# A three-part model on one core: the compressed attention layers rebuilt (order of the weight chunks, values as the stationary side, probabilities normalised one step ahead, norms from token sums)

## Chip, cores, metric

One core of one Trainium2 chip. The metric is the device time of one execution in microseconds; 3497.52 us is the median of three executions of the kernel before (3493.31 to 3498.54).

## What is computed

x has 512 tokens of 1024 features. Two layers of a first block (a gated mixer with attention, a linear attention layer, each with a feed-forward part) are followed by two layers of a second block. Only the middle part of a second-block layer matters here:

```python
x = x + 0.5 * rms(swiglu(rms(x), ...))                  # feed-forward 1
h = hybrid_mixer(rms(x))
x = x + rms(h)
x = x + 0.5 * rms(swiglu(rms(x), ...))                  # feed-forward 2

def hybrid_mixer(h):
    q, kc, vc, ks, vs, kw, vw, gates, bg, cg, xc = split(h @ w_in)
    # q: 8 heads x 64, in 2 groups of 4; each k, v: 2 groups x 64; bg, cg, xc: 512
    kc, vc = compress(kc), compress(vc)   # 31 blocks of 32 tokens: gelu(block @ w1) @ w2
    o_cmp = softmax(q . kc, blocks that ended) @ vc
    o_slc = softmax(rope(q) . rope(ks), causal) @ vs     # all 8 blocks are selected at 512 tokens
    o_win = softmax(rope(q) . rope(kw), causal) @ vw     # window of 512 tokens
    attn = g0 * o_cmp + g1 * o_slc + g2 * o_win          # g = sigmoid(gates)
    conv = bg * conv3(cg * xc)
    return concat(rms(attn), rms(conv)) @ w_out
```

## The kernel before

Everything is kept transposed: features on the 128 partitions, 512 tokens along them. A weight matrix is cut into chunks of 1024 x 256. SyncE loads chunks into a ring of four (line 2277); ACT rounds each into a high part (`split_next`, line 631), GpSimd subtracts for the low part (`low_part`, line 2297) and TensorE makes three products for each of 8 row tiles and 2 column tiles, 48 in all (`chunk_products`, line 451). h is split into high and low in the same way. ACT asks for its splits in an order that is written out by hand, two chunks ahead of TensorE, so a wait ahead of a split in ACT's queue holds the ring. A result sits in one of two two-bank PSUM buffers (`ps`) until DVE has taken it (`take`, line 1999); two more double banks (`mp`, single banks `m[0]` to `m[3]`) are for the rest.

The norm of x is not applied to h: its reciprocal root multiplies the results. Token sums of the squares (line 484) give a column, ACT takes the root, DVE the reciprocal and four diagonal tiles (line 748), and products with ones spread it over the partitions (line 500). `first_chunk` (lines 540 to 544) multiplies one chunk while the tiles of h arrive; the feed-forward layers use `first_pair` (lines 520 to 525), two chunks at once, the second into `mp[1]`.

`nsa_tensor`, `nsa_scalar` and `nsa_vector` are the compressed attention layer on TensorE, ACT and DVE. ACT first issues seven DMAs (lines 1860 to 1866), for which it waits until x is complete. The chunks then come in this order: kc/vc, ks/vs, cg/xc twice (columns 0 to 255, then 256 to 511), q first half, compression of k (two chunks, line 1621), kw/vw, q second half, bg twice, compression of v, gates (one column tile, 24 products), w_out. Between them stand the rotations (`turn_k`, `turn_q`, line 1660), transposes of v (`turn_v`, line 1653), the conv in DVE's `conv`, and the conv half's norm, made with wide products against ones (line 1852).

The attention itself runs in 24 steps over (query tile i, head pair m, branches): tiles 3 and 2 take one branch a step with 128(i+1) keys for each of two heads, tiles 1 and 0 both branches. In a step TensorE makes scores (line 1676) and adds the mask (line 1680), DVE finds the row maximum (line 2177), ACT the exponential (line 1962), TensorE transposes the probabilities (line 1692), ACT copies the first head's from PSUM (line 1971) and DVE the second's (line 2199), and TensorE multiplies with the values (line 1710):

```python
last = pe.matmul(out[:, u * (HD + 1):(u + 1) * (HD + 1)],
                 c.b_pT[:, s % 2, hh, t * P:(t + 1) * P], c.b_va[:, br, j, hh, :], ...)
```

The transposed probabilities are the stationary side; the values carry a column of ones, so that column 65 is the denominator. DVE's `combine` divides, gates and adds into token-major `b_o`. Turns lag scores by one step, values by two. At the end ACT squares each tile of `b_o` with an accumulated sum (lines 1981, 1984), and diagonal tiles turn, scale and transpose it back by products (line 1833) for the output projection (line 1820).

The first block's attention (line 956) has the values as stationary side already: for each tile j, head 0 into output partitions 0 to 63, then head 1 into 64 to 127. Its exponentials write a sum with `accum_out` (line 980). Lines 1098 and following have the same shape, one head after the other.

## Time and profile before

| what | value |
|---|---|
| median of three executions | 3497.52 us |
| the profiled execution | 3496.36 us |
| its span, first to last instruction | 3494.6 us |
| mean granted TensorE clock | 0.969 |
| TensorE, GpSimd, DVE, ACT busy | 3322.8, 1449.9, 1220.3, 1145.4 us |
| first compressed attention layer, h arriving to last step | 1702.0 to 1984.5 us |
| the second one's steps | 2961.7 to 3060.1 us (98.4, the first one's 97.7) |

Times inside are microseconds from the start of the span. A matmul with float32 operands is recorded as two matmuls; a record lasts longer than the distance to the next, because matmuls overlap, so distances between starts are what counts. The granted clock is 1.00 at 2.4 GHz and 0.50 at 1.2 GHz.

### The profile page before, as it was taken

To read this page: it belongs to the slowest core of one execution; us is meant where nothing else is said; L and a number is where in the kernel's file an instruction comes from. 1 tells how busy PE (TensorE), PEld (TensorE's weight loads), DVE (VectorE), ACT (ScalarE), POOL (GpSimd) and SP (SyncE) were. 2 spreads that over 40 slices of the span, in tenths; PEclk is the share of its full clock that TensorE was granted. 3 is DMA by queue.
4 is the path that set the end of the run, shared out by engine and by line. 5 is a ranking of instruction groups with operands and counts; after the bars stand their busy time and mean duration, and the time that the engine had idled before them with its cause. 6 is when DMAs were issued, how large, how long until landed. Compare 5 with 4: busy or idle time off the path is not lost.

```text
span 3494.6 us, 38964 instructions
## 1 busy us (share of the span) xinstructions
PE 3322.8 (95%) x15612; PEld 2716.9 (78%) x15612; DVE 1220.3 (35%) x1681; ACT 1145.4 (33%) x1203; POOL 1449.9 (41%) x1112
## 2 busy tenths in 40 slices
PE   8869999988799999999889999999999989999998
PEld 7638888866588888888777888888888767888887
DVE  6243432132643311220544652214221363752212
ACT  4244432241243323322323443223332223433321
POOL 4204554522155445445353054444544355035443
PEclk9959999988899999999999999999999999999999
DMA  4102222311022232222222022232222223012222
GB/s 147 63 0 85 96 96 107 104 71 60 24 97 96 96 109 97 96 96 103 100 97 73 9 89 96 96 109 86 97 97 105 85 94 121 1 73 96 96 97 96
DMA packets 46224, 302.04 MB, mean 86 GB/s; under 512 B 5392, under 2 KB 7696, under 8 KB 10784
## 3 DMA queue, kind: packets, MB, share of 16 engines
q1 hardware_dynamic: 41040, 292.79, 23.4%
q10 hardware_dynamic: 5072, 7.57, 0.7%
q8 instruction: 93, 1.52, 0.2%
q14 instruction: 19, 0.16, 0.0%
HBM read 296.15 MB, written 2.10 MB: 85 GB/s over the span
## 4 chain that ended last, share of the span: by engine, by line
PE 90%; DVE 5%; issue 3%; ACT 2%; ACTq 0%; DMA 0%; DVEq 0%; SPq 0%
PE main L451 73%; PE misc L1710 2%; PE main L561 2%; PE main L1820 1%; PE main L1676 1%; PE misc L1692 1%; PE main L1621 1%; PE main L520 1%; DVE diag L748 1%; PE main L521 1%; PE main L525 1%; PE misc L520 1%; PE misc L521 1%; PE misc L525 1%; PE main L1680 1%
## 5 line engine op out<-in xcount | busy, mean ns | idle before, releaser
L2297 POOL TENSOR_TENSOR w_lo<-stage,w_hi 128x512 fp32r<-128x512 f32 x1104 | 1444.6, 1341 | 2008.7 <-ACT w_hi L631 2008.5
L451 PE MATMUL main<-h_hi,w_lo 128*128 128x512 f32 x2616 | 1032.4, 395 | 18.9 <-DVE b_u L1999 18.9
L451 PE MATMUL main<-h_lo,w_hi 128*128 128x512 f32 x2616 | 1024.0, 391 | 0.0
L451 PE MATMUL main<-h_hi,w_hi 128*128 128x512 f32 x2616 | 1023.8, 391 | 0.0
L631 ACT ACTIVATE w_hi<-stage 128x2048 fp32r<-128x2048 f32 x276 | 525.2, 1910 | 462.3 <-DMA stage<-in_w 447.6
L451 PEld LDWEIGHTS main<-h_hi,w_lo 128*128 128x128 f32 x2616 | 495.6, 189 | 128.8 <-DVE b_u L1999 19.4
L451 PEld LDWEIGHTS main<-h_lo,w_hi 128*128 128x128 f32 x2616 | 495.7, 189 | 104.8 <-issue 2.4
L451 PEld LDWEIGHTS main<-h_hi,w_hi 128*128 128x128 f32 x2616 | 494.8, 189 | 104.2
L451 PE MATMUL main<-hid_hi,w_lo 128*128 128x512 f32 x1168 | 455.6, 390 | 0.2 <-DVE hid_lo L1537 0.2
L451 PE MATMUL main<-hid_lo,w_hi 128*128 128x512 f32 x1168 | 454.6, 389 | 0.0
L451 PE MATMUL main<-hid_hi,w_hi 128*128 128x512 f32 x1168 | 454.5, 389 | 0.0
L451 PEld LDWEIGHTS main<-hid_hi,w_lo 128*128 128x128 f32 x1168 | 219.5, 188 | 46.8 <-issue 0.7
L451 PEld LDWEIGHTS main<-hid_lo,w_hi 128*128 128x128 f32 x1168 | 219.4, 188 | 46.2 <-issue 0.5
L451 PEld LDWEIGHTS main<-hid_hi,w_hi 128*128 128x128 f32 x1168 | 219.4, 188 | 45.3
L820 DVE TENSOR_TENSOR val<-main,rstd 128x1024 f32<-128x1024 f32 x60 | 73.4, 1224 | 460.8 <-PE main L451 460.8
L800 DVE TENSOR_TENSOR gate<-main,rstd 128x1024 f32<-128x1024 f32 x66 | 80.8, 1224 | 318.0 <-PE main L451 301.2
L684 ACT ACTIVATE hid_hi<-val 128x1024 f32 (+1 forms) x66 | 69.9, 1059 | 370.6 <-DVE val L826 370.6
L853 DVE TENSOR_SCALAR y<-main,par 128x512 f32<-128x512 f32 x48 | 36.0, 750 | 389.8 <-PE main L451 330.7
L830 DVE TENSOR_TENSOR hid_lo<-val,hid_hi 128x1024 f32 (+1 forms) x66 | 89.5, 1356 | 91.1 <-ACT hid_hi L684 91.1
L679 ACT ACTIVATE sq<-gate 128x1024 f32<-128x1024 f32 x44 | 46.7, 1061 | 186.7 <-DVE gate L818 186.2
L845 DVE TENSOR_TENSOR x<-main,x 128x1024 f32<-128x1024 f32 x16 | 19.6, 1224 | 240.6 <-PE main L451 240.6
L1962 ACT ACTIVATE b_p<-main,b_nmax 128x512 f32<-128x512 f32 (+3 forms) x128 | 58.7, 525 | 92.2 <-DVE b_nmax L2177 92.2
(364 smaller groups left out, 3012.9 us busy)
## 6 DMA issues: line engine op xcount, KB each, us to landing
stage<-in_w SPq DMA_DIRECT2D x276, 1024.0 KB, 4.8
x<-in_xT SPq DMA_DIRECT2D x4, 512.0 KB, 8.3
out_x<-x ACTq DMA_DIRECT2D x4, 512.0 KB, 2.7
stage<-in_w SPq DMA_DIRECT2D x4, 256.0 KB, 8.4
b_r<-sq ACTq DMA_DIRECT2D x4, 256.0 KB, 3.5
b_r<-sq ACTq DMA_DIRECT2D x4, 255.5 KB, 4.5
ev_ws<-in_ev_ws ACTq DMA_DIRECT2D x1, 512.0 KB, 3.6
b_pos<-in_pos ACTq DMA_DIRECT2D x2, 256.0 KB, 4.7
```

The costliest lines, as they stand in the source:

```text
L451: last = pe.matmul(acc[:, m, :], w[a], r[b], start=start and k == 0 and j == 0, stop=stop and k == nk - 1 and j == 2)
L520: pe.matmul(accs[j][:, m, :], w[1], c.h_hi[:, k, :], start=k == 0, stop=False)
L521: pe.matmul(accs[j][:, m, :], w[0], c.h_hi[:, k, :], start=False, stop=False)
L525: last = pe.matmul(accs[j][:, m, :], c.w_hi[:, slots[j], k, m * P:(m + 1) * P], c.h_lo[:, k, :], start=False, stop=k == KT - 1)
L561: last = pe.matmul(acc[:, m, :], w[a], r[b], start=start and k == 0 and j == 0, stop=k == nk - 1 and j == 2)
L631: act.activation(c.w_hi[:, s, :, :].rearrange("p k n -> p (k n)"), c.stage[:, s, :], ACT.Copy)\
L684: e.activation(two(c.hid_hi, i), c.val[:, :, :], ACT.Copy).then_inc(c.hid_hi_done, 1)
L800: e.tensor_tensor(c.gate[:, :, 2:], c.ps[n.slot()][:, :, :], rstd, ALU.mult)\
L820: e.tensor_tensor(c.val[:, :, :], (c.mp[1] if extra else c.ps[n.slot()])[:, :, :], rstd, ALU.mult)\
L830: e.tensor_tensor(two(c.hid_lo, i), c.val[:, :, :], two(c.hid_hi, i).bitcast(F32), ALU.subtract).then_inc(c.hid_lo_done, 1)
L1710: last = pe.matmul(out[:, u * (HD + 1):(u + 1) * (HD + 1)], c.b_pT[:, s % 2, hh, t * P:(t + 1) * P], c.b_va[:, br, j, hh, :], start=brs[0] ...
L2297: last = e.tensor_tensor(c.w_lo[:, s, k:k + 2, :].rearrange("p k n -> p (k n)"), c.stage[:, s, k * CW:(k + 2) * CW], c.w_hi[:, s, k:k + 2, ...
```

## The change

- Chunks: kc/vc, cg first half, ks/vs, xc first half, compression of k, q first half, compression of v, kw/vw, gates, q second half, cg and xc second halves, bg twice, w_out with its first 512 rows reordered. The first two go through `first_pair`. ACT's splits and the steps of DVE and TensorE are reordered to match. `b_h` and `b_u` get two buffers.
- Values: `b_va` (64 columns, no ones) is the stationary side, the transposed probabilities stream, two heads go to the two halves of the output partitions, and all steps of a query tile and its compressed part add up in one PSUM bank.
- Probabilities: the exponential writes the denominators (`accum_out`), DVE's `shares` scales the probabilities by gate / denominator before their transposes. Turns lag scores by two steps, values by three. Both heads' copies are ACT's. A group of steps ends with one copy and two squares on ACT.
- Norms of both halves: token sums, root, diagonal tiles and a spread, the conv half's inside the steps.

```diff
-        self.b_p, _ = at("b_p", [2, 2, T], M2)
+        self.b_p, _ = at("b_p", [3, 2, T], M2)
-        self.b_va, _ = at("b_va", [2, TT, 2, HD + 1], MH)
+        self.b_va, _ = at("b_va", [2, TT, 2, HD], MH)
...
     def values(s):
...
+        pe.wait_ge(c.a_copied, 50 * l + 2 * s + 4)
+        for r, br in enumerate(brs):
+            for j in range(i + 1):
+                t = r * (i + 1) + j
+                for hh in range(2):
+                    last = pe.matmul(c.m[2 + i % 2][HD * hh:HD * hh + HD, m * P:(m + 1) * P],
+                                     c.b_va[:, br, j, hh, :], c.b_pT[:, s % 2, hh, t * P:(t + 1) * P],
...
+    def compressed_values(i):
...
+        for m in range(4):
+            for hh in range(2):
+                pe.matmul(c.m[2 + i % 2][HD * hh:HD * hh + HD, m * P:(m + 1) * P], c.b_vbd[:, hh, m, :],
+                          c.b_pcT[:, hh, i * P:(i + 1) * P], start=m == 0, stop=False)
+    def half_sums():
+        pe.wait_ge(c.half_sq, n(c.half_sq, 2))
+        for k in range(4):
+            last = token_sums(pe, c.m[2], c.ones, (c.sq, c.val)[k // 2][:, k % 2, :], k == 0, k == 3)
...
+    first_pair(pe, n, c, [group_slot(pe, n, c), extra_slot(n, c)])
+    chunk_products(pe, n, c, slot_after_extra(pe, n, c), c.h_hi, c.h_lo, KT, at={1: lambda: spread(pe, n, c)})
+    chunk_products(pe, n, c, slot_after_extra(pe, n, c), c.h_hi, c.h_lo, KT)
     pe.wait_ge(c.turn_loaded, 16 * (l + 1))
     turn_k()
     turn_v()
+    compressed(0)
+    z()
+    pe.wait_ge(c.tok_copied, n(c.tok_copied))
+    compressed_turn(0)
+    compressed(1)
+    rope_was_read()
+    turn_q(0)
+    compressed_out(0)
+    z()
...
+    z()
+    pe.wait_ge(c.a_gate_exp, l + 1)
+    turn_q(1)
+    rope_was_read()
+    pe.wait_ge(c.tok_copied, n(c.tok_copied))
+    compressed_scores()
+    z()
+    compressed_prob_turn()
     z()
     z()
...
+    for s in range(N_STEPS + 3):
         if s < N_STEPS:
             scores(s)
+        if s == 3:
+            half_sums()
+        if s == 6:
+            half_spread()
+        if 2 <= s < N_STEPS + 2:
+            turn(s - 2)
+        if s >= 3:
+            if group_starts(s - 3):
+                compressed_values(STEPS[s - 3][0])
+            values(s - 3)
...
+    half(accs[0], slots[0], 4, True, False, at={6: o_sums})
     pe.wait_ge(c.w_lo_done, n(c.w_lo_done))
+    half(accs[1], slots[1], 4, True, False, at={5: o_spread})
...
     split_next(act, n, c)
+    split_next(act, n, c)
     norm_copy(act, n, c)
-    split_next(act, n, c)
...
+    split_next(act, n, c)
+    split_next(act, n, c)
+    trig(c.b_cos)
     rounded(0)
     split_next(act, n, c)
     rounded(1)
+    token_values(0)
+    split_next(act, n, c)
+    gelu(0)
+    split_next(act, n, c)
+    trig(c.b_sin)
...
+    for s in range(N_STEPS + 4):
+        if s >= 4 and group_ends(s - 4):
...
+            act.activation(c.b_oT[:, :, i * P:(i + 1) * P], bank, ACT.Copy)
+            for j in range(2):
+                last = act.activation((c.sq, c.val)[j][:, :, i * P:(i + 1) * P], bank[:, 2 * j:2 * j + 2, :],
+                                      ACT.Square)
...
+        if 2 <= s < N_STEPS + 2:
...
+            for hh in range(2):
+                act.wait_ge(c.a_probT, 50 * l + 2 * s - 2 + hh + 1)
+                act.activation(c.b_pT[:, (s - 2) % 2, hh, 0:w], c.m[hh][:, 0:w], ACT.Copy).then_inc(c.a_copied, 1)
...
+                                   ACT.Exp, bias=c.b_nmax[:, s % 4, u:u + 1],
+                                   accum_out=c.b_den[:, s % 4, 2 * hh + br:2 * hh + br + 1]).then_inc(c.a_prob, 1)
+        if s == 2:
+            act.wait_ge(c.conv_done, n(c.conv_done))
+            for j in range(2):
+                act.activation((c.sq, c.val)[j][:, :, :], c.b_y[:, 2 * j:2 * j + 2, :], ACT.Square)\
+                    .then_inc(c.half_sq, 1)
+        if s == 4:
+            act.wait_ge(c.half_ssq, n(c.half_ssq))
+            act.activation(c.col[:, 0:4], c.m[2][:, 0:4], ACT.Sqrt, bias=c.eps, scale=1.0 / 512)\
+                .then_inc(c.half_std, 1)
...
     norm_recip(dve, n, c)
     take(c.sq[:, :, :])
     signal(c.kc_taken)
+    take(c.b_u[0][:, :, :], extra=True)
...
     dve.wait_ge(c.pairs_loaded, n(c.pairs_loaded, 64))
     flat(0)
+    flat(1)
+    take(c.val[:, :, :])
+    conv(0)
+    hidden(0)
+    angle(c.b_sin, 0.0)
...
+    take(c.b_u[1][:, :, :])
+    rope_q(1)
...
+    def shares(s):
...
+        dve.wait_ge(c.a_prob, 64 * l + exps_until(s + 1))
...
+        step(dve.reciprocal(den, den))
+        step(dve.tensor_tensor(den, den, gate, ALU.mult))
+        for hh in range(2):
+            for r, br in enumerate(brs):
+                p = c.b_p[:, s % 3, hh, r * w:(r + 1) * w]
+                u = 2 * hh + br
+                last = dve.tensor_scalar(p, p, c.b_den[:, s % 4, u:u + 1], None, ALU.mult)
+            last.then_inc(c.a_norm, 1)
```

## Rows read from the trace of the kernel before

**Rows 1.** The page, busy time, share of the span and instructions of each engine.
```profile
PE 3322.8 (95%) x15612; PEld 2716.9 (78%) x15612; DVE 1220.3 (35%) x1681; ACT 1145.4 (33%) x1203; POOL 1449.9 (41%) x1112
```

**Rows 2.** Stretches: start, end, length, busy time by engine, granted clock, DMA share, GB/s.
```profile
1731.98:1886.80 154.82, 142.69 (x698) 115.85 (x696) 72.86 (x87) 44.23 (x42) 80.73 (x57) 0.95 0.30 103
1886.80:1984.53 97.73, 92.44 (x699) 76.74 (x698) 71.05 (x144) 47.46 (x105) 4.01 (x4) 0.98 0.03 11
1984.53:2011.38 26.85, 26.85 (x129) 22.67 (x130) 9.01 (x21) 9.64 (x12) 7.16 (x6) 0.95 0.11 40
```

**Rows 3.** The chain of waits, in order of time: start, length, what.
```profile
1807.09 5.62 PE main L1621 x48
...
1814.43 10.90 PE main L451 x48
...
1872.00 3.45 PE misc L1852 x8
```

**Rows 4.** Timeline, front of the first layer: start, length, instructions, idle before and releaser.
```profile
1701.99 0.47 PE L540 MATMUL main<-h_hi,w_lo 128*128 128x512 f32 x1 [0.34 <-ACT h_hi L730]
...
1720.09 0.95 PE L484 MATMUL misc<-ones,acc 128*128 128x1 f32 x8
...
1724.14 1.91 ACT L631 ACTIVATE w_hi<-stage 128x2048 fp32r<-128x2048 f32 x1 [6.96 <-issue]
...
1726.13 4.92 POOL L2297 TENSOR_TENSOR w_lo<-stage,w_hi 128x512 fp32r<-128x512 f32 x4 [38.40 <-ACT w_hi L631]
...
1726.45 4.68 DVE L748 TENSOR_SCALAR diag<-ident,col 128x128 f32<-128x128 f32 x4
```

**Rows 5.** Timeline, front of the feed-forward layer behind it, TensorE.
```profile
2040.29 0.47 PE L520 MATMUL main<-h_hi,w_lo 128*128 128x512 f32 x1 [0.34 <-ACT h_hi L730]
...
2063.07 0.40 PE L451 MATMUL main<-h_hi,w_lo 128*128 128x512 f32 x1
```

**Rows 6.** Timeline, the long wait of the projections on three engines.
```profile
1763.28 0.60 ACT L1885 ACTIVATE b_va<-misc 128x512 f32<-128x512 f32 x1 [9.81 <-PE misc L1653]
...
1766.70 1.37 DVE L2057 TENSOR_TENSOR b_a_lo<-b_flat,b_a_hi 128x992 fp32r<-128x992 f32 x1 [11.91 <-ACT b_a_hi L1890]
...
1772.72 0.79 PE L451 MATMUL main<-h_hi,w_lo 128*128 128x512 f32 x1 [9.48 <-DVE b_u L1999]
```

**Rows 7.** Timeline, a step of query tile 3, and one of tile 1 on ACT.
```profile
1911.79 1.26 ACT L1962 ACTIVATE b_p<-main,b_nmax 128x512 f32<-128x512 f32 x2 [2.31 <-DVE b_nmax L2177]
...
1912.94 0.60 ACT L1971 ACTIVATE b_pT<-misc 128x512 f32<-128x512 f32 x1
...
1913.06 1.13 PE L1676 MATMUL main<-b_k,b_qr 64*128 64x512 f32 x4
...
1914.39 1.06 PE L1692 MATMUL misc<-ident,b_p 128*128 128x128 f32 x8
...
1915.29 1.90 PE L1710 MATMUL misc<-b_va,b_pT 128*128 128x65 f32 x16
...
1917.12 1.13 PE L1676 MATMUL main<-b_k,b_qr 64*128 64x512 f32 x4
...
1962.28 1.57 ACT L1962 ACTIVATE b_p<-main,b_nmax 128x256 f32<-128x256 f32 x4 [1.79 <-DVE b_nmax L2177]
```

**Rows 8.** Groups by line and shape over 1720 to 2023: count, busy us, mean ns, idle before.
```profile
L1710 PE MATMUL misc<-b_va,b_pT 128*128 128x65 f32 x320 | 38.6, 272 | 0.4 <-issue 0.4
```

**Rows 9.** Timeline and a stretch (last row), the first block's attention and mixing.
```profile
168.68 1.34 PEld L1098 LDWEIGHTS misc<-ev_ws,ev_vntok 128*64 128x64 f32 x16 [0.18 <-DVE val L1238]
...
256.73 0.18 ACT L980 ACTIVATION_READ_ACCUMULATOR score<-score,stat 128x1 f32 x1
...
261.56 1.09 PE L956 MATMUL misc<-probT,vs 128*64 128x128 f32 x16 [0.74 <-ACT probT L987]
262.59 0.50 PE L451 MATMUL main<-hid_hi,w_lo 128*128 128x512 f32 x1
...
183.00:262.00 79.00, 56.58 (x288) 31.95 (x290) 32.83 (x162) 35.40 (x93) 0.00 (x0) 0.58 0.00 0
```

More of the change, by code:

```diff
@@ L1661, in turn_q, with rope_was_read, gates_turn @@
         last.then_inc(c.rope_ps, 1)
+    def rope_was_read():
+        pe.wait_ge(c.rope_read, n(c.rope_read))
+    def gates_turn():
+        pe.wait_ge(c.gates_taken, n(c.gates_taken))
+        for t in range(TT):
+            last = pe.transpose(c.m[1][:, t * 24:(t + 1) * 24], c.acc[0:24, 0, t * P:(t + 1) * P],
+                                c.ident[0:24, 0:24])
+        last.then_inc(c.gates_turned, 1)
     def scores(s):
@@ new lines, in half_sums, with half_spread @@
+    def half_sums():
+        pe.wait_ge(c.half_sq, n(c.half_sq, 2))
+        for k in range(4):
+            last = token_sums(pe, c.m[2], c.ones, (c.sq, c.val)[k // 2][:, k % 2, :], k == 0, k == 3)
+        last.then_inc(c.half_ssq, 1)
+    def half_spread():
+        pe.wait_ge(c.half_diag, n(c.half_diag))
+        for i in range(TT):
+            last = pe.matmul(c.m[2][:, i * P:(i + 1) * P], c.ones[:, :], c.diag[:, i, :], start=True, stop=True)
+        last.then_inc(c.half_spread, 1)
+    first_pair(pe, n, c, [group_slot(pe, n, c), extra_slot(n, c)])
@@ L1815, in half @@
+        if 2 <= s < N_STEPS + 2:
[4 more added lines that the diff above has]
+            values(s - 3)
+    def half(acc, s, k0, start, stop, at={}):
         for k in range(k0, k0 + 4):
+            if k in at:
+                at[k]()
             for m in range(2):
@@ L1822, in half, with o_sums, o_spread @@
         return last
+    def o_sums():
+        pe.wait_ge(c.a_oT, 4 * l + 4)
+        for k in range(4):
+            last = token_sums(pe, c.m[0], c.ones, (c.sq, c.val)[k // 2][:, k % 2, :], k == 0, k == 3)
+        last.then_inc(c.half_ssq, 1)
+    def o_spread():
+        pe.wait_ge(c.half_diag, n(c.half_diag))
+        for i in range(TT):
+            last = pe.matmul(c.m[1][:, i * P:(i + 1) * P], c.ones[:, :], c.diag[:, i, :], start=True, stop=True)
+        last.then_inc(c.half_spread, 1)
     c.result_slot[post] = n.slot()
@@ L1845, in nsa_tensor @@
     last_sums(pe, n, c)
-def half_norm_tensor(pe, n, c):
-    for j in range(2):
-        pe.wait_ge(c.half_sq, n(c.half_sq))
-        for k in range(2):
-            last = pe.matmul(c.m[0][:, :], c.ones[:, :], (c.sq, c.val)[j][:, k, :],
-                             start=j == 0 and k == 0, stop=j == 1 and k == 1)
-    last.then_inc(c.half_ssq, 1)
 def nsa_scalar(act, n, c, l, norm, post, a, out):
@@ L2081, in hidden, with gated @@
         signal(c.cmp_taken)
-    def conv_gate(j):
-        take(c.val[:, :, :])
+    def gated(j):
         y = c.b_y[:, 2 * j:2 * j + 2, :]
@@ L2173, in nsa_vector @@
+    for s in range(N_STEPS + 1):
         if s < N_STEPS:
@@ new lines, in nsa_vector @@
+            signal(c.conv_done)
+        if s >= 1:
+            shares(s - 1)
+        if s == 5:
+            dve.wait_ge(c.half_std, n(c.half_std))
+            step(dve.reciprocal(c.col[:, 0:4], c.col[:, 0:4]))
+            for i in range(TT):
+                last = dve.tensor_scalar(c.diag[:, i, :], c.ident[:, :], c.col[:, i:i + 1], None, ALU.mult)
+            last.then_inc(c.half_diag, 1)
+        if 7 <= s < 9:
+            if s == 7:
+                dve.wait_ge(c.half_spread, n(c.half_spread))
+            x = c.b_y[:, 2 * s - 14:2 * s - 12, :]
+            dve.tensor_tensor(x, x, over_tiles(c.m[2][:, :]), ALU.mult).then_inc(c.half_done, 1)
```

450 lines of the change are left out of this document (153 added, 297 removed).

## The prediction

> **What bounds the kernel now.** I began with the page: TensorE is busy for 95% of the span and every other engine for 41% or less [rows 1]. So time comes back only where TensorE does less, works at the lower clock level or stands still. The change touches the two compressed attention layers alone, so next I cut the first of them into stretches: the projections before the attention steps, the 24 steps, and the first part of the output projection [rows 2]. The projections last 154.8 us with TensorE busy for 142.7 (12.1 us of standing still) at a mean granted clock of 0.95. The steps last 97.7 us with 92.4 busy at 0.98. The tail has no standing still. The second layer runs the same code with the same shapes. One execution of a layer is therefore 280 us of TensorE's queue, and twice anything found there is the answer.
>
> The chain of waits gives prices: 48 products of a weight chunk take 10.90 us (0.227 us each), the two compression chunks together 5.62, the conv half's norm through four wide ones-products 3.45 [rows 3].
>
> **Front of the layer.** Today one chunk is multiplied while h arrives. TensorE starts it at 1702.0; ACT issues seven DMAs after x is complete and splits the next chunk only at 1724.1; GpSimd makes its low part from 1726.1 in 4.92 us; DVE's four diagonal tiles take 4.68 us, ending at 1731.1, and the norm is spread by 1732.0 [rows 4]. Until then TensorE has done 66 products (48, and 18 of the second chunk). The change takes two chunks at once, as the feed-forward layers do: there the pair runs from 2040.3 to 2063.1, 22.8 us, with the sums inside [rows 5]. So here TensorE is through at 1702.0 + 22.8 = 1724.8, with 96 products done. But the third chunk is the one that ACT splits at 1724.1 behind its DMAs, and its low part is ready at 1726.1 + 4.9 = 1731.0: 6.2 us of standing still. Then 6 products (2.6 us, since it restarts at the lower level) and the spread (about 1.4): 1735.0. ACT now splits two chunks ahead of the square root, which moves the diagonals 1.9 us later, to 1733.0, still ahead of the spread. Net: the mark is 3.0 us later, with 102 products behind it and not 66; the 36 extra are 8.2 us. Gain 5.2 us. What the feed-forward layer has and this one doesn't is the ready third chunk; I do not give it that.
>
> **From the norm to the first step.** The 154.8 us hold one long wait, 9.48 us before the products of line 451, released by DVE's b_u. Behind it is a circle: DVE had waited 11.91 us for ACT's rounding of the compression blocks, and ACT was held 9.81 us in its order at the transposed values of TensorE's line 1653 [rows 6]. The change breaks this: both roundings stand ahead of the transposed values in ACT's queue and both compressions' inputs ahead of the sine angles in DVE's. So the 9.5 us go, and with them about 1.5 us of lower clock behind the pause. Work: 154.8 less 12.1 of standing still less about 4.7 lost at the lower level (0.95 over the stretch) is 138.0. From this go the 36 products that are now ahead of the mark (8.2) and the wide norm products (3.45); the turn of the compressed probabilities comes in (0.9). That is 127.2. What is late next? Walking the queues with the rows' durations I find: the second compression chunk of v or the key products near 1780, where GpSimd has 5.3 us a chunk and TensorE eats two in 5.62 (0 to 2 us); the values' transposes behind ACT's four copies (0.6); and the compressed scores, which wait for DVE's last rotation, itself behind the conv input that is now taken just before (2.0 to 2.6). With some lower clock I put 5 us: 132.2, ending 132.2 + 3.0 = 135.2 after today's mark. Against 154.8 the gain is 19.6 us, the front's 5.2 included.
>
> The cover for the compression is the weight ring. Splits are now asked for in pairs on ACT, and two compressions stand with only one 48-product chunk between them. Five chunks cost GpSimd 5 x 5.3 = 26.5 us while TensorE works about 2.8 x 4 + 11 x 2 = 33: it holds, with some 1 us of margin at the tightest.
>
> **The 24 steps.** A step of the last query tile runs 1913.06 to 1917.12, 4.06 us, TensorE never standing: scores and mask 1.33, transposes 0.90, values 1.83 [rows 7]. Values change form: now 128 columns of probabilities are loaded and 65 columns streamed; then 64 columns of values are loaded and 128 streamed, two heads into the two halves of the output partitions. The first attention layer already does this: 16 records from 261.56 to the next product at 262.59, 1.03 us. The same 64-column load without the alternation took 1.34 us of loads for 16 records. These are the two ends; I take the first, the same form in the same order [rows 9]. Saved: (1.83 - 1.03) / 16 x 320 records = 16.0 us a layer [rows 8]. The Trainium skill (TensorEngine Tiling (Array Packing), Key Properties) says that a change of tiling mode drains TensorE, which speaks against the change, since the values become a third form in each step. The row of 1.03 us already holds one such change at its end, so the trace bears the rule out only as something below 0.2 us a step.
>
> Other work of TensorE there: compressed values become 32 small products, 4 x 1.03 = 4.1 for 3.4 today; the conv norm now stands inside as 16 token sums, four of which take about 0.8 us [rows 4], so 3.3, and a spread of 0.9; the turn leaves (0.9). Busy today 92.4, less 2.0 for the lower level, is 90.5; so 90.5 - 16.0 + 0.7 + 4.2 - 0.9 = 78.5.
>
> That would be 19 us of gain, and I don't expect most of it. ACT gets DVE's half of the copies (about 12.7 us), 64 accumulator reads at 0.19 [rows 9] (12.2), the squares of the conv half (2.1), copies and squares of four groups (7), and two function table loads in step 4 (2.6). A step of tile 3 costs ACT two exponentials (1.26, 0.38 for reads) and two copies (0.55 apiece, a little under the row's 0.60, since they overlap), 2.7 in all, against TensorE's 3.26: covered. Tile 1: four exponentials took 1.57 [rows 7]; 2.4 with reads, and copies 1.1: 3.5 against 3.5. Tile 0: 2.7 against 2.2: ACT is the bound. DVE has 2.6 at most. TensorE's pauses in the walk: 2.0 at the third scores, 3.5 at the token sums (they wait for ACT's squares, which wait for DVE's gating), 0.7 at the spread, 3.3 spread over the ACT-bound steps, 5.0 in the longer drain (values now three steps behind scores). Together 14.5; with 1 us of clock the steps last 94.0 against 97.7. Gain 3.7 us.
>
> **Tail.** 16 wide products become 16 sums and a spread (3.3 + 0.9 for 3.6). DVE and ACT then make four tiles of hid in turn, each 1.4 us, as fast as TensorE takes them. Loss 0.5 us.
>
> **Sum.** 19.6 + 3.7 - 0.5 = 22.8 a layer, 45.6 for two. The profiled execution took 3496.4 us (span 3494.6), 1.2 below the median of three, 3497.5; so about 3451 for that, the forecast of the likeliest case.
>
> **Rivals.** (a) *The steps stay at ACT's or the column form's pace.* At 1.34 us for the values form, the walk gives 3 us more a layer; if an accumulator read costs 0.3 and not the 0.23 of the walk, 3.3 more. One or both: 3451 + 6 to 13, about 3462, and the steps give nothing. For: ACT is level with TensorE in eight steps. Against: row of 1.03. (b) *The ring starves.* DVE and GpSimd hold each other up more; my walk lengthens each DVE operation on SBUF beside GpSimd by 1.0 us (a diagonal tile beside it takes 4.68 / 4 = 1.17 us [rows 4]); with 1.4 it gives 6.7 us more a layer: 3464. (c) *The queues fit better.* No pause at the sums, reads hidden: the steps take 86, the projections 130: 10 us less a layer, 3431. (d) *The clock falls in the steps: slower.* The first attention layer, with the same pattern of short pauses, ran its 79 us at 0.58 [rows 9], most of it at 1.2 GHz, against 2.4 GHz in today's steps. If the new pauses (15% of the stretch, where today's are 5%) do this, the 78.5 us of work double. The point from which it decides is 22.8 / 78.5 = 29% of the work at the lower level, which eats the gain; all of it, with the 14.5 us of pauses swallowed by the longer work, makes 2 x (78.5 - 14.5 - 22.8) = 82 more than today, 3579. For: that row. Against: today's last steps pause too and stay near full clock. (e) *The order gives nothing*, because a new wait of 13 us takes the place of the b_u wait and the steps gain nothing: 2 x (19.6 - 13) = 13, 3484.
>
> **How the numbers follow.** Forecast 60%, (a) 12%, (b) 8%, (c) 9%, (d) 5%, (e) 6%. A measurement of this kernel can tell about 0.2%, 7 us, from no change. Faster holds all but (d) and part of (e): 0.91; same 0.04, slower 0.05. The range takes in (a), (b) and most of (c), and the bounds of the values form: 3430 to 3474.
>
> **What would show it.** Right: no wait above 3 us for b_u or val before line 451; about 6 us of standing still ahead of the third chunk; first step's scores 17 to 22 us earlier relative to the layer's start; value records 0.06 us apart; steps of tile 3 at 3.3 us, of tile 0 released by ACT; clock 0.95 or more. Wrong: TensorE released by GpSimd's low parts in the middle; a granted clock near 0.5 in the steps; steps of tile 3 released by ACT.

## The result, and the profile after

The changed kernel takes 3465.4 us, median of four runs (3463.1 to 3465.9), against 3498.0 for the kernel before: a ratio of 0.9909, 95% interval 0.9895 to 0.9922, a gain of 32.6 us. The forecast was 3451, the range 3430 to 3474. The direction is right and the range holds it; 14 us of the forecast gain are missing. The number by itself doesn't choose between the forecast and its rivals: it lies nearer to (a), about 3462, and (b), 3464, than to 3451. What chooses is the profile, and the runs further down.

The page of the changed kernel, to be read against [rows 1]:

```profile
span 3463.6 us, 39458 instructions
...
PE 3308.1 (96%) x15788; PEld 2697.2 (78%) x15788; DVE 1205.3 (35%) x1689; ACT 1185.4 (34%) x1395; POOL 1447.2 (42%) x1112
```

TensorE's busy time fell by 14.7 us and its standing still from 171.8 to 155.5, by 16.3. The stretches of the first compressed layer, cut at the same events as [rows 2] with the front ahead of them (start, end, length, busy time of PE, PEld, DVE, ACT and POOL, granted clock, DMA share, GB/s):

```profile
1701.24:1734.46 33.22, 26.88 (x118) 22.13 (x119) 21.95 (x31) 12.73 (x14) 8.95 (x8) 0.90 0.26 90
1734.46:1874.96 140.50, 133.62 (x663) 108.87 (x661) 77.92 (x90) 43.93 (x45) 79.07 (x57) 0.96 0.30 105
1874.96:1966.81 91.85, 87.50 (x777) 65.21 (x777) 60.02 (x150) 67.00 (x196) 0.00 (x0) 0.93 0.04 13
1966.81:1994.83 28.02, 28.02 (x138) 23.80 (x137) 7.86 (x15) 8.75 (x12) 7.03 (x6) 0.94 0.10 38
```

| us, first layer | before | forecast | after |
|---|---|---|---|
| first h product to the spread norm | 30.0 | 33.0 | 33.2 |
| from there to the first scores | 154.8 | 132.2 | 140.5 |
| the 24 steps | 97.7 | 94.0 | 91.9 |
| tail | 26.9 | 27.4 | 28.0 |

From one layer's first h product to the next's it is 322.65 and 323.25 us in the two layers, 15.65 and 14.60 less than before; forecast was 22.8. The projections are short by 8.3, the tail by 0.6, and the steps give 2.1 more.

TensorE's waits of the first layer, timeline of the changed kernel (start, length, group, idle time ahead of it and its releaser):

```profile
1730.58 0.76 PE L444 MATMUL main<-h_hi,w_lo 128*128 128x512 f32 x1 [6.34 <-POOL w_lo L2276]
...
1764.10 0.50 PE L444 MATMUL main<-h_hi,w_lo 128*128 128x512 f32 x1 [2.02 <-DVE val L2004]
...
1781.77 0.33 PE L1612 MATMUL main<-w_hi,b_a_lo 128*62 128x256 f32 x1 [1.68 <-POOL w_lo L2276]
...
1788.58 0.47 PE L444 MATMUL main<-h_hi,w_lo 128*128 128x512 f32 x1 [1.10 <-POOL w_lo L2276]
...
1833.88 4.72 PE L1715 MATMUL misc<-b_kc,b_q 64*128 64x32 f32 x64 [1.45 <-DVE b_qr L2040]
...
1879.33 1.13 PE L1676 MATMUL main<-b_k,b_qr 64*128 64x512 f32 x4 [1.41 <-ACT b_p L1971]
...
1886.92 2.28 PE L477 MATMUL misc<-ones,sq 128*128 128x1 f32 x13 [1.85 <-ACT val L1978]
```

The 9.48 us for b_u [rows 6] are gone; instead of it four short waits stand in the projections, 6.25 us, and 0.6 in two smaller ones. Behind the wait for val, behind the one for b_qr and in the first steps the granted clock is lower for a while. Behind the two waits for GpSimd's low parts it is not: it stays at 1.00 from 1776 to 1836, and in the second layer, where the first of them is 2.74 us long, from 2837 to 2852 too. The same kernel in finer stretches:

```profile
1764.00:1768.00 4.00, 3.90 (x11) 3.03 (x12) 3.89 (x4) 0.72 (x1) 4.00 (x3) 0.60 0.58 236
1776.00:1836.00 60.00, 55.15 (x292) 43.65 (x292) 24.97 (x32) 20.73 (x24) 43.01 (x32) 1.00 0.35 123
1836.00:1842.00 6.00, 6.00 (x38) 5.26 (x37) 2.40 (x3) 0.00 (x0) 0.00 (x0) 0.54 0.00 0
1842.00:1850.00 8.00, 8.00 (x34) 6.51 (x34) 4.45 (x5) 2.86 (x2) 4.69 (x3) 0.92 0.00 0
1887.00:1892.00 5.00, 5.00 (x27) 5.00 (x28) 0.51 (x2) 0.00 (x0) 0.00 (x0) 0.57 0.01 3
1892.00:1897.00 5.00, 5.00 (x34) 4.67 (x36) 0.00 (x0) 2.50 (x6) 0.00 (x0) 0.50 0.00 0
1897.00:1966.00 69.00, 68.34 (x680) 50.87 (x676) 49.51 (x131) 57.01 (x175) 0.00 (x0) 0.99 0.01 2
```

A step of query tile 3, as in [rows 7]:

```profile
1901.64 1.13 PE L1676 MATMUL main<-b_k,b_qr 64*128 64x512 f32 x4
1902.70 0.44 PE L1680 MATMUL main<-b_mask,b_identr 128*128 128x128 f32 x2
1902.97 1.06 PE L1691 MATMUL misc<-ident,b_p 128*128 128x128 f32 x8
1903.96 1.09 PE L1702 MATMUL misc<-b_pT,b_va 128*64 128x128 f32 x16
1904.99 1.13 PE L1676 MATMUL main<-b_k,b_qr 64*128 64x512 f32 x4
```

3.35 us instead of 4.06: values 1.03 instead of 1.83, transposes 0.99 instead of 0.90.

### The profile page after: what moved, and what is told of

Same layout as the page of the kernel before. It is cut to its first block, busy times and chain, and to the rows that moved or that the text cites. A ratio compares the mean times of both kernels' runs of the same rounds, so it can differ in the third digit from the quotient of the medians.

```text
span 3463.6 us, 39458 instructions
## 1 busy us (share of the span) xinstructions
PE 3308.1 (96%) x15788; PEld 2697.2 (78%) x15788; DVE 1205.3 (35%) x1689; ACT 1185.4 (34%) x1395; POOL 1447.2 (42%) x1112
## 4 chain that ended last, share of the span: by engine, by line
issue 49%; POOL 32%; PE 17%; DVE 1%; ACT 1%; POOLq 0%; DMA 0%; ACTq 0%; DVEq 0%; SPq 0%
POOL w_lo L2276 32%; PE main L444 12%; PE main L1815 1%; PE main L554 1%; PE main L1676 1%; PE misc L1702 1%; PE misc L1691 0%; PE misc L477 0%; DVE h_lo L2337 0%; PE main L1680 0%; DMA stage<-in_w 0%; PE misc L1715 0%; ACT b_p L1971 0%; DVE y L879 0%; POOLq L2274 0%
## 5 line engine op out<-in xcount | busy, mean ns | idle before, releaser
L444 PE MATMUL main<-h_hi,w_lo 128*128 128x512 f32 x2584 | 1017.9, 394 | 17.3 <-POOL w_lo L2276 13.9
L444 PE MATMUL main<-h_lo,w_hi 128*128 128x512 f32 x2584 | 1012.0, 392 | 0.0
L444 PE MATMUL main<-h_hi,w_hi 128*128 128x512 f32 x2584 | 1011.7, 392 | 0.0
L819 DVE TENSOR_TENSOR val<-val,sq 128x1024 f32<-128x1024 f32 x66 | 86.4, 1309 | 7.8
```

The lines of the kernel that those rows point to most:

```text
L444: last = pe.matmul(acc[:, m, :], w[a], r[b], start=start and k == 0 and j == 0, stop=stop and k == nk - 1 and j == 2)
L819: e.tensor_tensor(c.val[:, :, :], c.val[:, :, :], c.sq[:, :, :], ALU.mult)\
```

## The experiments

Each run changes the kernel after the change in one place, conv_late in two (it holds take_early's early value chunk) and best_four in four. Medians are compared with its 3465.4 us; the layer columns are the distance of first h products in the profiled run.

| run | median, us | ratio to before (95%) | layer 1 | layer 2 |
|---|---|---|---|---|
| the change | 3465.4 | 0.9909 (0.9895 to 0.9922) | 322.65 | 323.25 |
| splits_first | 3447.8 | 0.9863 (0.9848 to 0.9878) | 315.76 | 313.79 |
| take_early | 3467.4 | 0.9917 (0.9903 to 0.9932) | 322.77 | 323.42 |
| conv_late | 3454.6 | 0.9878 (0.9862 to 0.9893) | 315.73 | 317.36 |
| scores_late | 3457.5 | 0.9895 (0.9880 to 0.9910) | 319.29 | 316.97 |
| sums_late | 3459.9 | 0.9895 (0.9880 to 0.9910) | 318.84 | 317.37 |
| best_four | 3425.2 | 0.9796 (0.9782 to 0.9811) | 304.63 | 303.41 |
| undo_pair | 3474.1 | 0.9934 (0.9920 to 0.9947) | 326.06 | 326.56 |
| token_form | 3501.1 | 1.0014 (1.0003 to 1.0026) | 341.42 | 346.09 |
| heads_outer | 3480.3 | 0.9954 (0.9942 to 0.9967) | 331.50 | 328.82 |
| copy_in_four | 3463.5 | 0.9916 (0.9900 to 0.9931) | 326.13 | 320.66 |
| fill_pause | 3462.2 | 0.9896 (0.9880 to 0.9911) | 321.94 | 317.95 |
| fill_whole | 3467.5 | 0.9910 (0.9894 to 0.9927) | 322.56 | 324.13 |

A single layer of a single profile scatters with the clock: in copy_in_four the part ahead of the steps, where nothing differs, took 177.3 us against 173.7, at 0.92 against 0.95. So the medians judge and the profiles say where. The executions of one kernel lie 3 to 16 us apart, and an interval reaches some 5 us either way, so a difference of 2 or 3 us between medians says nothing.

**splits_first: ScalarE's splits ahead of its DMA issues.**

```diff
+    split_next(act, n, c)
+    split_next(act, n, c)
+    n.skip(c.acc_ready, 2)
+    norm_std(act, n, c)
     act.wait_ge(c.nsa_free, n(c.nsa_free))
     act.dma_start(c.b_pos[:, :], a["pos"]).then_inc(c.pos_loaded, 16)
...
-    split_next(act, n, c)
-    split_next(act, n, c)
-    norm_copy(act, n, c)
+    act.wait_ge(c.spread_ready, n(c.spread_ready))
+    act.activation(c.rstd[:, :], c.m[1][:, :], ACT.Copy).then_inc(c.rstd_copied, 1)
```

> The changed kernel with ScalarE's two weight splits (and the square root) put ahead of its wait for the layer's memory and its seven DMA issues. Theory (the front's pause is ScalarE's order, nothing else): ScalarE stood 7.09 us ahead of the split at 1723.52, so the splits come some 7 us earlier, GpSimd's low part of the third chunk too, and TensorE's wait for it (6.34 us in layer 1, 5.38 in layer 2) is gone but for up to 0.5 us in front of the spread: 11 us less, 3454 against 3465. Rival (GpSimd and the ring of weight buffers set the pace, so that time won in one place is lost in the next wait for a low part): the pause at the third chunk shrinks and the waits for w_lo near 1781 and 1788 grow by as much; 3463 to 3466. Rival 2 (TensorE's granted clock gives back what the pause cost, the chip allowing only so much work): the pause goes and the share of the higher clock in the layer falls; less than half of the 11 us.

17.6 us less, more than the 11 expected. The pause is gone and with it the low clock of the front, which the 11 had left out: the norm is spread 25.4 us after the first h product, in both layers, and not 33.2 and 32.6. In the run:

```profile
1724.00:1728.00 4.00, 4.00 (x19) 3.33 (x20) 2.77 (x4) 0.60 (x1) 2.22 (x2) 1.00 0.90 329
1728.00:1730.60 2.60, 2.60 (x14) 2.13 (x13) 2.43 (x9) 0.31 (x2) 0.00 (x0) 1.00 1.03 340
1730.60:1733.00 2.40, 2.40 (x12) 2.01 (x11) 2.30 (x4) 2.40 (x3) 0.00 (x0) 1.00 1.03 220
```

The changed kernel has 0.24 us of TensorE in the first of these stretches, 0.02 in the second, and in the third a clock of 0.50. Both rivals fall: the waits for w_lo further on grew by only 0.5 us (2.17 and 1.11 in layer 1), and the wait for val from 2.02 to 3.22, which is far less than the 7.8 us won in front of them; and the clock of the steps didn't fall, it rose (0.94 for 0.93).

**take_early and conv_late: VectorE's order.** The diff is that of take_early; in conv_late `conv(0)` stands further down, between `hidden(1)` and `rope_q(0)`.

```diff
     flat(0)
+    take(c.val[:, :, :])
     flat(1)
-    take(c.val[:, :, :])
-    conv(0)
     hidden(0)
+    conv(0)
     angle(c.b_sin, 0.0)
```

> The changed kernel with VectorE's order in the projections altered: the gate's value chunk is scaled out of PSUM after the first of the two flattening groups instead of after both, and the first compressed hidden group is taken before the convolution instead of after it. Theory (the 8.3 us by which the projections missed the forecast are short waits on in-order neighbours, and a lower clock behind each): the wait for val at 1764.10 (2.02 us; 1.38 in layer 2) goes, with it the low clock behind it (that chunk took 12.71 us against 10.93, 1.8 us); the GELU is no longer 8.64 us late, so the split behind it is 5 us or more earlier and TensorE's waits for GpSimd's w_lo near 1781 and 1788 (1.68 and 1.10 us; 2.74 and 1.10 in layer 2) go too: 5 to 7 us a layer, 3452 to 3456. Rival (GpSimd's pace): the w_lo waits stay, only the first wait and its clock go: 3 us a layer, 3459. Rival 2 (the clock's loss is not tied to these waits): val's wait goes but the low stretch turns up elsewhere: 1.5 to 4 us in all.

> Like the run with the value chunk taken early, where the wait of 2.02 us for val went and one of 3.47 us for the scaled queries came in its place, but with the convolution's first half (some 9 us of VectorE) put behind the scaling of the queries and the second hidden group. Theory (between 1745 and 1787 VectorE's own chain is the bound, and what is moved inside it only moves the wait): with 9 us taken out of the chain both waits go, and the low clock behind the first (1.8 us): 3.5 to 4.5 us a layer, 3456 to 3458; GpSimd's two waits (2.0 and 1.1 us) stay. Rival (the convolution is then late for the rotation of the queries and the second turning of the keys, near 1805): a new wait of 2 to 4 us there, 3462 to 3466.

take_early gave nothing, which neither theory nor rivals had. The wait for val and its low clock went, but in its place:

```profile
1787.55 3.75 PE L1650 MATMUL misc<-b_q,b_turn 128*128 128x512 f32 x4 [3.47 <-DVE stat L2011]
```

With the convolution taken out of the chain (conv_late) this wait is gone too, the one for val doesn't return, and 10.8 us are won, more than the 8 expected. So VectorE's chain from the flattening to the scaled queries was the bound there, and shuffling inside it only moved the wait. Of the 10.8 us, 5.0 are waits (the projections' are 2.0 and 3.0 us shorter in the two layers). Most of the rest is clock, and not all of that can be laid to the edit: behind the wait for b_qr, 1.45 us as before, the low stretch of its first layer is half as long. GpSimd's two waits stayed (1.77 and 1.34). No new wait stands near 1805.

**scores_late: compressed scores one chunk later.** ScalarE's third split goes ahead of its exponential of them.

```diff
     turn_q(1)
+    z()
     rope_was_read()
     pe.wait_ge(c.tok_copied, n(c.tok_copied))
     compressed_scores()
     z()
     compressed_prob_turn()
     z()
-    z()
```

> The changed kernel with the compressed scores and the transposes of their probabilities one chunk later on TensorE, so that VectorE's rotation of the second half of the queries is over before the scores want the bank. Theory: the wait of 1.45 us for b_qr (both layers) goes and the clock no longer falls behind it (scores 4.65 against 3.70 before the change, masks 1.02 against 0.57, the chunk 12.66 against 10.93: 3.1 us); if all of that is tied to the wait, 4.5 us a layer, 3456. Rival (the scores themselves, narrow products of 32 columns, lower the clock behind them, not the wait): 1.5 us a layer, 3462. Rival 2 (the later end of VectorE's work on the compressed probabilities delays the convolution and the last two scalings out of PSUM): a new wait in front of the first scores or of the last chunk, 3465 or more.

7.9 us less, between the two prices. The wait is gone, the scores take 3.69 us instead of 4.65. In the first layer the clock still falls behind them, for a shorter time:

```profile
1842.00:1848.00 6.00, 6.00 (x72) 5.33 (x71) 0.00 (x0) 0.00 (x0) 0.56 (x1) 0.89 0.49 175
1848.00:1856.00 8.00, 8.00 (x32) 6.51 (x32) 6.67 (x8) 1.06 (x1) 0.00 (x0) 0.87 0.01 2
```

Counting 1 minus the granted clock times the length, that is 1.7 us lost against 3.4 in the two stretches from 1836 to 1850 of the changed kernel. In the second layer it doesn't fall at all (1.00 from 2899 to 2913). So the low stretch doesn't need the wait, since it can come without it, here and in both layers of best_four; what share the narrow products have in it isn't settled.

**sums_late: the convolution half's norm two steps later.**

```diff
-        if s == 3:
+        if s == 5:
             half_sums()
-        if s == 6:
+        if s == 8:
             half_spread()
```

ScalarE's and VectorE's parts of it move by two steps as well.

> The changed kernel with the convolution half's token sums, spread, scaling and low parts two steps later in the attention loop. Theory (the one long pause in the steps, 1.85 us for val in front of the sums, 2.49 in layer 2, is the squares not being ready at the fourth step): the pause is gone or under 0.3 us and the low clock of 1887 to 1897 with it: 2 us and some 2 of clock a layer, 3457. Rival (the low clock is brought on by the first steps themselves, which follow the chunks, with small products): only the pause goes, 3461. Rival 2 (ScalarE is the bound of the first steps): the pause moves to the next step's exponentials, 3465.

5.5 us by the medians, between the prices of theory and rival. The wait for val is gone; the steps last 88.44 and 88.42 us in the two layers, for 91.85 and 93.46. A low stretch at the first steps remains (0.72 from 1886 to 1892), shorter than before, but a second one stands around the sums' new place:

```profile
1898.00:1908.00 10.00, 10.00 (x63) 8.45 (x63) 2.23 (x6) 2.53 (x6) 0.00 (x0) 0.66 0.00 0
```

So of the low clock the larger part moved along with the sums, and what went is mainly the wait.

**best_four: the four edits together** (splits_first, conv_late, scores_late, sums_late).

> The changed kernel with the four edits together: splits first, convolution late (with the early value chunk), scores late, sums late. Alone they gave, against the changed kernel's 3465.4: 17.6, 10.8, 7.9 and 5.5 us by the medians, 41.8 together. Theory (each removes a wait of its own and the lower clock behind it, in different places of the layer): they add up but for the clock of the first steps, which three of them counted as theirs (2.4 us in layer 2): 3424 to 3430. Rival (GpSimd's pace: with the layer's front 6 us earlier and the projections' waits gone, the low parts of the compressed and query chunks come late): two or more of the gains go into waits for w_lo, 3435 to 3445.

3425.2 us, as the theory had it: 40.2 less than the change, where the four alone sum to 41.8. What is left of waits for other engines in its first layer, up to the steps (timeline; beside them 1.02 us at 1747.28 that the profile puts down to no engine, and 0.28 for b_vbd):

```profile
1753.63 0.47 PE L444 MATMUL main<-h_hi,w_lo 128*128 128x512 f32 x1 [0.55 <-POOL w_lo L2279]
...
1769.74 0.33 PE L1612 MATMUL main<-w_hi,b_a_lo 128*62 128x256 f32 x1 [1.73 <-POOL w_lo L2279]
...
1776.24 0.47 PE L444 MATMUL main<-h_hi,w_lo 128*128 128x512 f32 x1 [1.35 <-POOL w_lo L2279]
...
1865.51 1.13 PE L1676 MATMUL main<-b_k,b_qr 64*128 64x512 f32 x4 [1.40 <-ACT b_p L1974]
```

This version beats both kernels, the one before by 2.0% (1.9 to 2.2). That the four nearly add up says that they stand in different places; it doesn't show each one's mechanism.

**undo_pair: the front as before.**

```diff
-    first_pair(pe, n, c, [group_slot(pe, n, c), extra_slot(n, c)])
-    chunk_products(pe, n, c, slot_after_extra(pe, n, c), c.h_hi, c.h_lo, KT, at={1: lambda: spread(pe, n, c)})
-    chunk_products(pe, n, c, slot_after_extra(pe, n, c), c.h_hi, c.h_lo, KT)
+    first_chunk(pe, n, c, group_slot(pe, n, c))
+    chunk_products(pe, n, c, group_slot(pe, n, c), c.h_hi, c.h_lo, KT, at=norm_hooks(pe, n, c))
+    z()
+    z()
...
```

ScalarE's copy of the spread and VectorE's second scaling move with it.

> The changed kernel with the front undone: one chunk alone under the activations, token sums and spread inside the second, VectorE's second scaling out of an ordinary bank, ScalarE's copy of the spread between its two splits. Theory: 36 of the 102 products that now lie ahead of the spread move behind it (8.2 us at 0.227 us each) and the pause ahead of the third chunk, with the low clock behind it, goes (the mark at 30.0 instead of 33.2 us after the first product): 5 us a layer more, 3475 against 3465. Rival (the pair is worth nothing, because GpSimd's low parts, which start as late either way, hand the gain back further on): within 2 us of 3465. Rival 2 (the front's pause is what the pair costs, and the undone form is the better one by it): 3455 to 3460.

8.6 us more, where 10 were expected: that bears out the front's term of 5.2 us a layer, as near as runs that scatter by 7 us can. In the profile the first scores come 3.4 and 5.3 us later after the first h product, and some of that is clock.

**token_form and heads_outer: the value products.** First token_form's edit, then the order of the loops in heads_outer.

```diff
-                    last = pe.matmul(c.m[2 + i % 2][HD * hh:HD * hh + HD, m * P:(m + 1) * P],
-                                     c.b_va[:, br, j, hh, :], c.b_pT[:, s % 2, hh, t * P:(t + 1) * P],
+                    last = pe.matmul(c.m[2 + i % 2][:, m * P + HD * hh:m * P + HD * hh + HD],
+                                     c.b_pT[:, s % 2, hh, t * P:(t + 1) * P], c.b_va[:, br, j, hh, :],
...
```

```diff
-        for r, br in enumerate(brs):
-            for j in range(i + 1):
-                t = r * (i + 1) + j
-                for hh in range(2):
+        for hh in range(2):
+            for r, br in enumerate(brs):
+                for j in range(i + 1):
+                    t = r * (i + 1) + j
```

> The changed kernel with the products of probabilities and values, and the compressed ones, in the form of the kernel before (probabilities stationary, 64 columns of values moving, tokens on the partitions of the output); copies and squares read the bank as they did, so what comes out is in another arrangement and only the time is of use. Theory (the steps are bound by TensorE, and the value form is worth 0.8 us for each 16 products, 1.83 against 1.03): 20 times 0.8 us, 16 us a layer more, less 0.1 us a step for the change of form that falls away: 13 to 16 us a layer, 3491 to 3498, the whole gain of the change again. Rival (ScalarE's copies and exponentials set the pace of the steps): the products grow but run in what were waits; 3 to 8 us a layer, 3471 to 3481.

> The changed kernel with the value products of a step in another order: all of the first head, then all of the second, instead of one head and the other in turn (the two write different halves of the output's partitions). Theory (the alternation is what gives 1.03 us for 16 records; without it the nearest row of the kernel before had 1.34 us of loads for 16): 0.3 us for each 16 records, 6 us a layer, 3477 to 3479 against 3465. Rival (the pace is that of one product, 128 columns streamed, whatever its place): no change, 3464 to 3467. Rival 2 (nothing at all overlaps without the alternation, and a product takes twice as long): 20 us a layer, 3505.

token_form costs 35.6 us, the whole gain and more; the rival (ScalarE sets the pace) falls. The profiled execution took 3508.9 us. The step's values take 1.82 us again, from 1906.84 to 1908.66. Part of the excess over 32 is clock. Stretches of its second layer's steps:

```profile
2963.00:2973.00 10.00, 8.98 (x46) 8.99 (x46) 0.90 (x3) 2.28 (x5) 0.00 (x0) 0.58 0.00 0
2973.00:2983.00 10.00, 10.00 (x42) 8.38 (x43) 1.34 (x3) 1.71 (x5) 0.00 (x0) 0.50 0.01 2
2983.00:2993.00 10.00, 10.00 (x43) 8.38 (x42) 4.30 (x13) 6.13 (x12) 0.00 (x0) 0.50 0.01 2
2993.00:3003.00 10.00, 10.00 (x54) 7.55 (x54) 2.44 (x6) 3.79 (x10) 0.00 (x0) 0.71 0.00 0
3003.00:3013.00 10.00, 10.00 (x83) 8.78 (x81) 8.50 (x17) 6.58 (x17) 0.00 (x0) 1.00 0.01 2
```

heads_outer costs 14.9 us, near the theory's 12 to 14. Its step:

```profile
1901.06 1.06 PE L1691 MATMUL misc<-ident,b_p 128*128 128x128 f32 x8
1902.05 1.58 PE L1702 MATMUL misc<-b_pT,b_va 128*64 128x128 f32 x16
1903.56 1.13 PE L1676 MATMUL main<-b_k,b_qr 64*128 64x512 f32 x4
```

1.51 us for the 16 records in place of 1.03: in a step of tile 3 the alternation of the two heads is worth 0.48 us of the form's 0.80. In a step of tile 2, with 12 records, it is 1.07 for 0.81, so the steps are 7.5 us longer in each layer and not 20 times 0.48.

**copy_in_four: does ScalarE bind the last steps?**

```diff
-    act.activation(c.b_pT[:, (s - 2) % 2, hh, 0:w], c.m[hh][:, 0:w], ACT.Copy).then_inc(c.a_copied, 1)
+    parts = 4 if s - 2 >= 16 else 1
+    for q in range(parts):
+        x = slice(q * w // parts, (q + 1) * w // parts)
+        last = act.activation(c.b_pT[:, (s - 2) % 2, hh, x], c.m[hh][:, x], ACT.Copy)
+    last.then_inc(c.a_copied, 1)
```

> The changed kernel with ScalarE's copies of the transposed probabilities cut into four instructions each in the last eight steps of a layer (what is copied is the same); by the distance of ScalarE's short instructions, some 0.2 us from one to the next, it adds about 0.35 us a copy, 0.7 us a step. Theory of the prediction (ScalarE is level with TensorE in these eight steps): all of it shows, 5.6 us a layer, 3476 against 3465. Theory from the profile after (ScalarE stands 0.46 to 0.68 us in each of these steps, waiting for TensorE's transposes): it fits but for 0 to 0.2 us a step, 1.6 us a layer at most, 3465 to 3469.

No change by the median (3463.5; six executions from 3460.1 to 3475.7, where 3476 was the bound case). The eight short copies took 1.27 us up to the next exponential where two long ones took 0.97, so 0.3 us were added a step and not the 0.7 planned; that fits into ScalarE's idle time: counted from the first of the last eight steps, the others start where they did, to 0.01 us, in both layers. What shows is behind the last scores, where ScalarE's copies, a table load of 1.28 us and TensorE's last products follow one another: TensorE's two waits there are 1.21 and 1.00 us, for 0.47 and 0.26, 1.5 us a layer. The bound case is refuted for 0.3 us a step, not beyond.

**fill_pause and fill_whole: the clock without the pause.** The diff is fill_pause's; fill_whole has 30 products. They stand ahead of the third chunk.

```diff
+    for _ in range(20):
+        pe.matmul(c.m[1][:, 0:P], c.ident[:, :], c.ones[:, :], start=True, stop=True)
     chunk_products(pe, n, c, slot_after_extra(pe, n, c), c.h_hi, c.h_lo, KT, at={1: lambda: spread(pe, n, c)})
```

> The changed kernel with 20 products of 128 columns, whose output nobody reads, put into TensorE's pause of 6.34 us ahead of the third chunk. No wait is taken away. Theory (a pause costs its own length and a stretch at the lower granted clock behind it; 1730.6 to 1734 runs at 0.50): the stretch behind the pause stays at 1.00 and 1.5 to 2 us a layer come back, 3461 to 3462, the pause's idle time being filled by work that does nothing. Rival (the clock is lowered for what the engine did over a longer time, pause or no pause): nothing, or the low stretch turns up later in the layer; 3465 or more.

> As the run with 20 idle products in the pause ahead of the third chunk, with 30 of them. The 20 took 4.63 us and left TensorE 2.00 us of waiting, and the six products behind it still ran at a granted clock of 0.52. Theory (any pause, even of 2 us, is followed by the low stretch; it is the pause and not the work that decides): with the pause closed the third chunk's first products run at 1.00 (0.227 us apart and not 0.43) and the layer's front is 1.5 us shorter than with 20; 3459 to 3463. Rival (the products of 128 columns don't count like the chunk's own, so that the clock falls behind them as behind a pause): the six products stay at 0.5, 3462 to 3466.

With 20 products 2.00 us of pause stayed, and the chunk's first products still stood 0.43 us apart in the first layer. In the second, behind 1.76 us of pause, they stood 0.23 apart, at full clock, so it isn't so that any pause of this size is followed by a low stretch:

```profile
2793.18 0.47 PE L444 MATMUL main<-h_hi,w_lo 128*128 128x512 f32 x1 [1.76 <-POOL w_lo L2278]
2793.49 0.40 PE L444 MATMUL main<-h_lo,w_hi 128*128 128x512 f32 x1
```

With 30:

```profile
1726.26 6.86 PE L1757 MATMUL misc<-ones,ident 128*128 128x128 f32 x60
1733.18 0.47 PE L444 MATMUL main<-h_hi,w_lo 128*128 128x512 f32 x1
1733.49 0.39 PE L444 MATMUL main<-h_lo,w_hi 128*128 128x512 f32 x1
1733.72 0.40 PE L444 MATMUL main<-h_hi,w_hi 128*128 128x512 f32 x1
...
1834.33 6.16 PE L1715 MATMUL misc<-b_kc,b_q 64*128 64x32 f32 x64 [1.45 <-DVE b_qr L2042]
```

The products behind it stand 0.23 us apart: with the pause closed, the clock stays up there. The spread norm comes 32.0 and 31.7 us after the first h product in the two layers, for 33.2 and 32.6. But the kernel is no faster (3467.5; with 20 products 3462.2, which is the number that the theory gave, but no more than the scatter away from 3465.4). TensorE's waits between there and the first scores grew by as much as the front had won, from 6.9 to 7.9 us and from 7.3 to 8.5. The compressed scores took 6.16 us where the changed kernel's took 4.72, but that row runs from 3.8 to 6.4 us from run to run behind the same wait of 1.45 us, so it can't be laid to the idle products. In these runs idle products bought nothing; doing away with the waits did.

## Why the prediction was right, and where its sizes were off

**Front.** The mark was forecast at 33.0 us and came at 33.2, with the pause of 6.2 at 6.34. undo_pair returned 8.6 of the 10.4 us that the term claims for two layers. What the prediction did not give the front, the ready third chunk, was there to be had by the order of ScalarE's queue alone: splits_first has the mark at 25.4.

**Projections: the term that was mis-sized is "With some lower clock I put 5 us: 132.2".** The b_u wait went as argued. Of the waits that the walk named, those for GpSimd were put at 0 to 2 us and measured 2.8, the one at v's transposes was put at 0.6 and measured 0.28, and the one at the compressed scores was put at 2.0 to 2.6 and measured 1.45. Missing from the walk was the wait for val, 2.02 us: the first query chunk needs the bank that VectorE frees only after both flattenings. With one of 0.33 for the scaled queries they make 6.9 us. The lower clock was all but left out: 0.96 over 133.6 us of busy time is about 5.3 us. Work is then 140.5 - 6.9 - 5.3 = 128.3 us, against 127.2 in the forecast. So of the 8.3 us missing, 7.2 are waits and clock (12.2 where 5 were forecast) and 1.1 are work. conv_late and scores_late took away val's and b_qr's waits and what follows them, and won 18.8 us for two layers by the two medians.

**Steps: near in the sum by errors that cancel, which is luck.** The forecast was 78.5 us of work, 14.5 of pauses and 1 of clock. Measured were 4.35 of pauses, about 0.07 x 87.5 = 6.1 of clock, and with these 81.4 of work. Each pause was put too long: 2.0 us at the third scores where 1.41 were measured, 3.5 at the token sums (1.85), 0.7 at the spread (0.15), 3.3 in steps bound by ACT (none), 5.0 in the drain (0.7). "Tile 0: ACT is the bound" was wrong. ScalarE's timeline in such a step of the changed kernel:

```profile
1957.25 0.39 ACT L1971 ACTIVATE b_p<-main,b_nmax 128x128 f32<-128x128 f32 x1
1957.50 0.23 ACT L1971 ACTIVATION_READ_ACCUMULATOR b_p<-main,b_nmax 128x1 f32 x1
1957.59 0.39 ACT L1971 ACTIVATE b_p<-main,b_nmax 128x128 f32<-128x128 f32 x1
1957.84 0.23 ACT L1971 ACTIVATION_READ_ACCUMULATOR b_p<-main,b_nmax 128x1 f32 x1
1958.54 0.66 ACT L1963 ACTIVATE b_pT<-misc 128x256 f32<-128x256 f32 x2 [0.46 <-PE misc L1691]
```

The next exponential starts 0.09 us after a read has, so a read of 0.23 costs 0.09 (the prediction charged 0.19, and 0.23 in its walk, where [rows 9] has a length of 0.18), and ScalarE then waits 0.46 for TensorE. The value form was worth what its row said, 1.03 us, and heads_outer shows that the other end of the bound, 1.34, would have been 1.51.

**The rule on changes of form.** The transposes, which stand between the scores and the values of 64 columns, take 0.99 us in the changed kernel and in heads_outer; in token_form, without that form, 0.89 (1910.00 to 1910.89). With six records in place of eight it is 0.77 for 0.68. So the change of form costs about 0.1 us a step, by this some 2.4 a layer, inside the forecast's bound of 0.2 and most of the 2.9 us by which the steps' work was undersized. The Trainium skill (TensorEngine Tiling (Array Packing), Key Properties) says that such a change drains TensorE; the trace agrees in that the change costs time, and has it at this small price.

**Tail.** 1.2 us of loss instead of 0.5; no run was made on it.

**Rivals.** (a) falls with copy_in_four and the 1.03 us, though its number was near. (b), the ring, is a small truth: 2.8 us of waits a layer, which no reordering here took away. Its condition, 1.4 us more for each VectorE operation beside GpSimd, isn't met: a diagonal tile takes 1.30 us beside it and 0.28 without, 1.0 more, as the forecast had it. (c) was half right, on the pauses of the steps, and failed on the projections; the queues do fit better, but only after four more edits. (d) held in part: the clock of the steps fell to 0.93, with 3.4 us near 0.5 behind the third scores and 10 us from 1887 on. That cost about 6 of some 81 us of work, 8%, far from the 29% at which it decides; token_form had about 34 us near 0.5 in one layer. (e) falls.

**Signs.** Borne out: no wait above 3 us for b_u or val, 6.34 us of standing still ahead of the third chunk, value records 0.06 us apart, 3.35 us for a step of tile 3. Not borne out: the first scores came 11.1 us earlier after the first h product, not 17 to 22; ScalarE holds up no step of tile 0, but for 0.26 us in the drain; the clock of the steps is 0.93. Two of its signs of being wrong came as well, weakly: TensorE was released by GpSimd's low parts in the middle (1.68 and 1.10 us), and the clock stood near 0.5 for some 10 us of the steps. The mechanism held, then, and the gain was oversized by 14 us.

What stays open: why the clock is low for 10 us in one run of the same steps and for less in another, and why it falls behind a wait of 2.02 us and not behind one of 2.74.

## What to carry to other kernels

When a reordering removes one long wait on in-order queues, expect short ones in its place on neighbours that have no slack, and walk the queue of every engine that has taken over work: the bank that a late read holds was the wait that was missed. Add a term for the lower clock beside the one for the pauses: here, from the spread norm to the last step, it cost about as much as they did (some 11.4 us for 11.2 in the first layer), though it didn't follow each of them. If moving an operation inside a busy engine's chain changes nothing, take it out of the chain.

## What the runs showed that was not expected

Many of VectorE's operations that read and write SBUF are slow while GpSimd runs, and at once quick when it stops. In take_early GpSimd's low parts end at 1779.45; VectorE's timeline:

```profile
1778.37 1.37 DVE L2020 TENSOR_SCALAR gate<-gate 128x512 f32<-128x512 f32 x1
1779.77 0.43 DVE L2021 TENSOR_SCALAR gate<-gate 128x512 f32<-128x512 f32 x1
```

The two do the same amount of work. It isn't the line either: in the kernel before line 2015 takes 1.41 us beside GpSimd and 0.43 without it, once each in both layers. Operations that read PSUM don't show it (line 2004 of the changed kernel, 1.22 to 1.23 us for b_q either way). It would fit with the waits that remain where GpSimd's low parts and VectorE's chain are both full, but no run here tests that.
